# Plain fp32 input and output projections, with seven modulation sums moved into the output projection

## Chip, core and metric

The kernel runs on one core of a Trainium2 chip. The metric is the device time of one execution in microseconds; several executions are timed and their median is taken.

## What is computed

One decoder layer over 256 tokens of width 2048, all in fp32. The parts that matter here, cut from the reference:

```python
mod = (silu(c) @ w_ada + b_ada)            # 6 parts of 2048: sh1, sc1, g1, sh2, sc2, g2
h = rmsnorm(x, norm1_g) * (1 + sc1) + sh1
proj = h @ w_in                            # 2048 -> 3904: sq, sk, sv (1024 each), cq 512, ckv 256, kr 64
sb_out  = stick_breaking_attention(sq, sk, sv)                 # 8 heads of 128
mla_out = mla_attention(rmsnorm(cq) @ w_uq, rmsnorm(ckv) @ w_ukv, kr)   # 8 heads
mixed = concat([rmsnorm(sb_out), rmsnorm(mla_out)]) @ w_o      # 2048 -> 2048
x = x + g1 * mixed
h2 = rmsnorm(x) * (1 + sc2) + sh2
x = x + g2 * peer_ffn(h2, ...)             # top-16 experts of 16384 per head and token
out = rmsnorm(x, final_norm_g)
```

## The kernel before

**Stages.** The order of the work on each engine is written out by hand. TensorE goes through: an opening, in which the first two modulation parts are summed and three column blocks of `w_in` (`cq`, `ckv`, `q0`, named `OPENING`) are multiplied in plain fp32 (L876, L882); the input projection proper, the five blocks `q1`, `k0`, `k1`, `v0`, `v1` of 512 columns each (L892 to L920); the latent products (L923 to L981, among them the plain fp32 products by `contract`, L457); attention, a software pipeline over 16 heads (`JOBS`), whose stages are `scores`, `middle`, `values` and `squares`; the output projection, four blocks `w_o0` to `w_o3` of 512 columns (L1055 to L1092); the query projection (L1134); and then the expert retrieval, which gathers rows of `peer_u` and `peer_v` by index and runs to the end.

**Split products.** In the input and the output projection an fp32 product is made from three fp32r products. A block of 16 chunks of 128 rows is handled in 8 pairs of chunks (`PAIRS`, class `Pair`). For each pair ScalarE casts the weights to fp32r (`make_high`, L448, into `win_high` or `wo_high`, four buffers each), VectorE subtracts that from the whole (`make_low`, L452, in place in the weight ring as `ring_low`), and the activations are parted likewise (`hT_high` L1322 and `hT_low` L1740; `mix_high_part` L1434 and `mix_low_part` L1874). TensorE then multiplies high by high, high by low and low by high: 24 matmuls of 256 columns per pair in `q1`, `k0` and `k1` (L912), 12 of 512 columns in `v0` and `v1` (L906) and in the output projection (L1069).

**Weights.** Block weights go through a ring of two slots of 32 KB per partition, loaded in halves by SyncE's DMA queue. A slot's half is loaded again when its reader has passed a semaphore (`plan_load`, `halves_read`).

**Modulation.** `w_ada` is 96 pieces of 1 MB. The first 32 (two parts) are summed in the opening (`first_step`, L486; pieces of 512 KB through 14 buffers, and SyncE's load of a piece waits for the step that frees its buffer). Pieces 32 to 95 are loaded by GpSimd's queue through three buffers (`ada_late`, L308) and each added on VectorE by one instruction of 128x2048 (`ada_sum`, L322). At the end of a part, TensorE sums it over the partitions with 16 one-column matmuls (`ada_cols`, L333), and VectorE may begin the next part only after these. In the kernel before, pieces 32 to 58 stand between the `make_low` calls of the input projection, 59 to 63 behind it, 64 to 70 (`ADA_IN` is 71) just ahead of attention on VectorE, and 71 to 85 in the output projection: two ahead of its loop, 13 in blocks 1 to 3.

**Rotary table.** VectorE makes the arguments of sine and cosine (L1659 to L1677) in the middle of the first 16 opening steps, and ScalarE's `Sin` (L1262) follows them ahead of the copies of the transposed `x`.

## Time and profile before

| | us |
|---|---|
| median of 3 executions | 1753.91 |
| lowest and highest | 1749.77 and 1756.27 |
| the profiled execution, whole | 1751.18 |
| its span, first to last instruction | 1749.4 |
| TensorE busy in the span | 1478.3 |
| VectorE busy | 1206.5 |
| ScalarE busy | 542.8 |
| GpSimd busy | 690.7 |
| mean granted clock of TensorE | 0.909 of 2.4 GHz |

A row of a timeline gives the start in us from the start of the span, the length in us, the engine, the line of the kernel, the operation, output and inputs by their names in the program, the shapes and the count; in brackets stands how long the engine was idle ahead of it and what ended that. A row of the chain of waits gives a start, a length and what the end of the program waited for in that stretch. The trace keeps two records for a plain fp32 matmul and one for an fp32r matmul; both print as f32. Lengths of matmuls overlap, so a rate is read from one start to the next.

### The profile page before, as it was taken

To read this page: it belongs to the slowest core of one execution; us is meant where nothing else is said; L and a number is where in the kernel's file an instruction comes from. 1 tells how busy PE (TensorE), PEld (TensorE's weight loads), DVE (VectorE), ACT (ScalarE), POOL (GpSimd) and SP (SyncE) were. 2 spreads that over 40 slices of the span, in tenths; PEclk is the share of its full clock that TensorE was granted. 3 is DMA by queue.
4 is the path that set the end of the run, shared out by engine and by line. 5 is a ranking of instruction groups with operands and counts; after the bars stand their busy time and mean duration, and the time that the engine had idled before them with its cause. 6 is when DMAs were issued, how large, how long until landed. Compare 5 with 4: busy or idle time off the path is not lost.

```text
span 1749.4 us, 20157 instructions
## 1 busy us (share of the span) xinstructions
PE 1478.3 (85%) x7320; PEld 980.5 (56%) x7320; DVE 1206.5 (69%) x2134; ACT 542.8 (31%) x1589; POOL 690.7 (39%) x626
## 2 busy tenths in 40 slices
PE   2979999989999998898999757656689899988874
PEld 2558987878788875666676434324333343333331
DVE  5877886879889988898454467768654555445463
ACT  3003442764311247343210146537421010101132
POOL 1000011000122354556676466555654454445461
PEclk9889999999999999999999876667789999998987
DMA  9999997849969679999999899998989999999996
GB/s 337 386 385 407 402 354 308 303 167 370 380 233 359 225 293 379 377 368 397 390 402 396 325 388 379 378 350 319 394 338 406 366 402 400 362 417 389 416 381 249
DMA packets 149806, 624.46 MB, mean 357 GB/s; under 512 B 33994, under 2 KB 38272, under 8 KB 86528
## 3 DMA queue, kind: packets, MB, share of 16 engines
q0 software_dynamic: 82976, 427.52, 62.6%
q1 hardware_dynamic: 66732, 195.67, 29.1%
q8 instruction: 58, 0.95, 0.2%
q14 instruction: 40, 0.33, 0.0%
HBM read 797.54 MB, written 2.10 MB: 457 GB/s over the span
## 4 chain that ended last, share of the span: by engine, by line
PE 31%; DMA 30%; DVE 24%; issue 6%; POOL 5%; ACT 3%; DVEq 1%; SPq 1%; POOLq 0%; ACTq 0%
DMA u_rows<-in_peer_u,expert 23%; DVE u_rows L2033 12%; PE ps L1167 6%; PE ps L1069 5%; PE ps L457 4%; PE ps L912 4%; DVE first_acc L486 3%; DMA v_rows<-in_peer_v,expert_rows 3%; POOL v_rows L801 3%; PE ps L906 2%; PE ps L1219 2%; PE ps L1134 2%; DMA ada_first<-in_w_ada 2%; PE ps L1204 2%; DMA u_rows<-in_peer_v,expert_rows 1%
## 5 line engine op out<-in xcount | busy, mean ns | idle before, releaser
L2033 DVE SCALAR_TENSOR_TENSOR u_rows<-u_rows,h 128x1024 f32<-128x1024 f32 (+1 forms) x416 | 595.3, 1469 | 377.9 <-DMA u_rows<-in_peer_u,expert 374.3
L801 POOL DMA_INDIRECT u_rows<-in_peer_u,expert x256 | 320.6, 1253 | 364.5 <-DVE u_rows L2033 289.5
L801 POOL DMA_INDIRECT v_rows<-in_peer_v,expert_rows x199 | 264.1, 1327 | 162.3 <-PE ps L1167 108.5
L1167 PE MATMUL ps<-v_rows,diag 128*32 128x512 f32 x1592 | 259.4, 693 | 65.1 <-DMA v_rows<-in_peer_v,expert_rows 35.6
L1219 PE MATMUL ps<-dense_rows,dense_weight 128*128 128x512 f32 x640 | 290.6, 612 | 14.9 <-DVE dense_sums L2112 8.2
L457 PE MATMUL ps<-h2T,dense_rows 128*128 128x256 f32 x1280 | 284.0, 383 | 4.2 <-ACT dense_weight L1565 4.1
L457 PEld LDWEIGHTS ps<-h2T,dense_rows 128*128 128x128 f32 x1280 | 243.4, 191 | 52.6 <-issue 17.9
L1219 PEld LDWEIGHTS ps<-dense_rows,dense_weight 128*128 128x128 f32 x640 | 123.1, 196 | 181.9 <-issue 174.9
L1167 PEld LDWEIGHTS ps<-v_rows,diag 128*32 128x32 f32 x1592 | 64.9, 125 | 182.5 <-issue 182.0
L308 POOL DMA_DIRECT2D ada_late<-in_w_ada x61 | 32.4, 531 | 303.7 <-DVE ada_acc L322 260.8
L1204 PE MATMUL ps<-high_hot,low_hot 128*128 128x40 f32 x512 | 82.1, 332 | 78.7 <-issue 54.0
L322 DVE SCALAR_TENSOR_TENSOR ada_acc<-ada_late,cact,ada_acc 128x2048 f32<-128x2048 f32 x57 | 133.8, 2348 | 18.8 <-DMA ada_late<-in_w_ada 17.7
L1167 PE MATMUL ps<-spare_rows,diag 128*32 128x512 f32 x296 | 135.7, 673 | 9.7 <-DMA v_rows<-in_peer_v,expert_rows 9.7
L1204 PEld LDWEIGHTS ps<-high_hot,low_hot 128*128 128x128 f32 x512 | 78.9, 244 | 95.0 <-issue 95.0
L1134 PE MATMUL ps<-h2T,ring 128*128 128x256 f32 x512 | 114.2, 383 | 0.0
L1134 PEld LDWEIGHTS ps<-h2T,ring 128*128 128x128 f32 x512 | 97.4, 192 | 13.0
L1487 ACT ACTIVATE hidden<-hidden 128x16 f32<-128x16 f32 x15 | 3.2, 215 | 314.6 <-DVE hidden L2041 311.5
L1576 ACT ACTIVATE low_hot<-iota,slot_rows 128x128 f32<-128x128 f32 x256 | 78.1, 387 | 41.1 <-PE ps L1204 40.9
L486 DVE SCALAR_TENSOR_TENSOR first_acc<-ada_first,cact,first_acc 128x1024 f32<-128x1024 f32 x60 | 77.0, 1284 | 16.1 <-DMA ada_first<-in_w_ada 10.8
L1509 ACT COPY weight_rows<-kept 32x4 f32<-32x4 f32 x240 | 47.1, 196 | 109.4 <-DVE kept L2058 106.7
L1561 ACT ACTIVATE diag<-ident,weight_rows 128x32 f32<-128x32 f32 x256 | 58.6, 308 | 40.0 <-PE ps L1167 39.4
L448 ACT CAST win_high<-ring 128x1024 fp32r<-128x1024 f32 x40 | 41.8, 1052 | 74.4 <-DMA ring<-in_w_in 32.0
(308 smaller groups left out, 1874.1 us busy)
## 6 DMA issues: line engine op xcount, KB each, us to landing
ada_late<-in_w_ada POOLq DMA_DIRECT2D x61, 1024.0 KB, 7.8
dense_rows<-in_dense_u SPq DMA_DIRECT2D x40, 1024.0 KB, 8.9
dense_rows<-in_dense_v SPq DMA_DIRECT2D x40, 1024.0 KB, 9.0
ada_first<-in_w_ada SPq DMA_DIRECT2D x64, 512.0 KB, 11.6
ring<-in_w_in SPq DMA_DIRECT2D x10, 2048.0 KB, 23.8
ring<-in_w_o SPq DMA_DIRECT2D x8, 2048.0 KB, 16.8
ring<-in_w_peer_q SPq DMA_DIRECT2D x8, 2048.0 KB, 13.8
opened<-in_w_in SPq DMA_DIRECT2D x8, 1024.0 KB, 13.0
```

Source lines behind the costliest of these rows:

```text
L322: nc.vector.scalar_tensor_tensor(out=a, in0=piece, scalar=cact[:, kc:kc + 1], in1=a, op0=ALU.mult, op1=ALU.add).then_inc(ada_steps, 1)
L457: ins = nc.tensor.matmul(half, lhs(k), rhs(k), start=(k == 0), stop=(k == kc - 1))
L486: nc.vector.scalar_tensor_tensor(out=a, in0=piece, scalar=cact[:, kc:kc + 1], in1=a, op0=ALU.mult, op1=ALU.add).then_inc(first_steps, 1)
L801: nc.gpsimd.indirect_dma_start(buf[:, :], None, table, bass.IndirectOffsetOnAxis(ap=places, axis=0), bounds_check=last_sparse, oob_is_err= ...
L912: ins = nc.tensor.matmul(banks[b // 2][:, T * (b % 2):T * (b % 2) + T], w.of(part, k, P * b, P), h[:, ch, :], start=first and b % 2 == 0, ...
L1069: ins = nc.tensor.matmul(banks[t], mixed[:, h, P * t:P * t + P], w.of(part, k), start=h % H == 0 and part is w.high and mixed is mix_high_ ...
L1134: ins = nc.tensor.matmul(bank[:, T * s:T * s + T], ring[item[name][0]][:, lo:lo + P], h2T[:, ch, :], start=(ch == 0 and s == 0), stop=(ch ...
L1167: ins = nc.tensor.matmul(ps[rows, k, :], diag[n % len(diag)][:, :], v_slot(n)[0][:, 512 * k:512 * k + 512], start=first, stop=last)
L1204: ins = nc.tensor.matmul(o, low_hot[i % 2][:, k, :], high_hot[i % 2][:, k, :], start=True, stop=True)
L1219: ins = nc.tensor.matmul(ps[:, 4 + t, :], weight_tile(PIECE * m + a)[:, P * t:P * t + P], rows[:, 512 * a:512 * a + 512], start=m == 0 and ...
L1576: ins = nc.scalar.activation(hot[:, k, :], iota128[:, :], ACT.Abs, scale=-1.0, bias=slot_rows[:, 1, BATCH * b + k:BATCH * b + k + 1])
L2033: ins = nc.vector.scalar_tensor_tensor(out=u_rows[b][:, lo:hi], in0=u_rows[b][:, lo:hi], scalar=1.0, in1=h2[:, q // H, lo:hi], op0=ALU.mul ...
```

## The change

1. **Plain fp32 products.** Class `Pair`, both sets of cast buffers, `ring_low`, the parted activations and all semaphores between them are gone. TensorE reads the ring and `hT` or `mix` directly: 64 matmuls per input block of 256 columns, 32 per block of 512 columns, and it waits itself for the weights' halves.
2. **Modulation.** `ADA_IN` is 64. Pieces 64 to 70 are summed in the output projection: the list of places there grows from 13 to 20 (`(0, 2)` to `(0, 7)` and `(1, 3)` are new). In the input projection the sums stand in a row.
3. **Attention's end.** The pipeline has 20 steps on TensorE, not 22; the squares of the last two heads follow the first two pairs of the output projection.
4. **Rotary arguments** go to the fourth step of the second 16 opening steps (`trig_args`), and `Sin` behind ScalarE's first part of `hT`.

```diff
-    def halves_read(high_read, n, last):
-
-        return (high_read, PAIRS * n + PAIRS // 2 + 1), unit_read(last)
...
-        plan_load(name, n % 2, halves_read(in_high_read, n, f"{name}_1"))
+        plan_load(name, n % 2, ((in_half_read, n + 1), unit_read(f"{name}_1")))
...
-        plan_load(f"w_o{n}", n % 2, halves_read(w_high_read, n, f"w{n}_1_1"))
+        plan_load(f"w_o{n}", n % 2, (unit_read(f"w{n}_0_1"), unit_read(f"w{n}_1_1")))
...
-    ADA_IN, ADA_OUT = 71, 86
+    ADA_IN, ADA_OUT = 64, 86
...
-                for m in range(PAIRS):
-                    w = Pair(name, PAIRS * n + m, m, win_high, width)
...
-                    pe.wait_ge(in_low, w.c + 1)
...
+                w = chunks(name)
+                for ch in range(KC):
+                    if ch % KH == 0:
+                        loaded(pe, name, ch // KH)
...
+                            ins = nc.tensor.matmul(banks[t][:, 0:width], hT[:, ch, P * t:P * t + P], w[:, ch, 0:width],
+                                                   start=(ch == 0), stop=last)
...
+                                ins = nc.tensor.matmul(banks[b // 2][:, T * (b % 2):T * (b % 2) + T],
+                                                       w[:, ch, P * b:P * b + P], hT[:, ch, :],
...
-            for k in range(JOBS + 6):
+            for k in range(JOBS + 4):
...
+                def product(h, t):
+                    ins = nc.tensor.matmul(banks[t], mix[:, h, P * t:P * t + P], w[:, h, :],
+                                           start=(h % H == 0), stop=(h % H == H - 1))
...
+                    if n == 0 and m < 2:
+                        squares(JOBS - 2 + m)
...
             for j in range(4):
                 gained(j)
                 move_h(2 * j)
-                if j:
-                    opened_read_through(dve, j - 1, 2)
-                    h_parted(j - 1)
                 if j < 3:
                     for kc in range(KC):
                         first_step(j + 1, kc)
+                        if j == 0 and kc == 3:
+                            trig_args()
...
-                    if (n, m) in ((1, 0), (1, 1), (1, 2), (1, 6), (1, 7), (2, 0), (2, 1), (2, 6), (2, 7), (3, 0), (3, 1), (3, 2), (3, 3)):
+                    if (n, m) in ((0, 2), (0, 3), (0, 4), (0, 5), (0, 6), (0, 7), (1, 0), (1, 1), (1, 2), (1, 3), (1, 6), (1, 7), (2, 0), (2, 1), (2, 6), (2, 7), (3, 0), (3, 1), (3, 2), (3, 3)):
                         ada_sum(next(ada))
```

Three places in the order of the instructions follow. `ps` is PSUM, a number behind a name is its buffer, `x8` counts like instructions in a row, and brackets hold the semaphores that a row waits for.

TensorE where attention ends and the output projection begins, before (`L1022` and `L1023` are the last values, `L1030` squares, `L1044` the rows of the gate):

```order
L1022 MATMUL ps<-ma_114,vm 128x256
L1023 MATMUL ps<-ma_114,vm 128x128
L1030 MATMUL ps<-ones,sq 128x1 x4
L1069 MATMUL ps<-wo_high_123,mix_high_part 128x512 x2
L1069 MATMUL ps<-wo_high_123,mix_low_part 128x512 x2
L1069 MATMUL ps<-wo_high_123,mix_high_part 128x512 x2
L1069 MATMUL ps<-wo_high_123,mix_low_part 128x512 x2
L1069 MATMUL ps<-ring_low_119,mix_high_part 128x512 x4
```

The same place in the changed kernel:

```order
L974 MATMUL ps<-ma_108,vm 128x256
L975 MATMUL ps<-ma_108,vm 128x128
L1011 MATMUL ps<-ring_49,mix 128x512 x4
L982 MATMUL ps<-ones,sq 128x1 x2
L1011 MATMUL ps<-ring_49,mix 128x512 x4
L982 MATMUL ps<-ones,sq 128x1 x2
L996 MATMUL ps<-ident,modc 128x128 x16
L1011 MATMUL ps<-ring_49,mix 128x512 x24
```

Twelve matmuls of a pair became four, they read the ring and `mix` themselves, and the last squares stand behind the first two pairs.

VectorE ahead of attention, before (`L343` adds the bias of the gate's part, `L1810` is attention's first instruction on this engine):

```order
L343 TENSOR_TENSOR modc<-ps,vcA 128x16 [waits ada_columns,qpe_ready]
L319 TENSOR_SCALAR ada_acc<-ada_late_87,cact 128x2048 [waits ada_columns,ada_late2_loaded]
L322 SCALAR_TENSOR_TENSOR ada_acc<-ada_late_85,cact,ada_acc 128x2048 [waits ada_steps,ada_late0_loaded]
L322 SCALAR_TENSOR_TENSOR ada_acc<-ada_late_86,cact,ada_acc 128x2048 [waits ada_steps,ada_late1_loaded]
L322 SCALAR_TENSOR_TENSOR ada_acc<-ada_late_87,cact,ada_acc 128x2048 [waits ada_steps,ada_late2_loaded]
L322 SCALAR_TENSOR_TENSOR ada_acc<-ada_late_85,cact,ada_acc 128x2048 [waits ada_steps,ada_late0_loaded]
L322 SCALAR_TENSOR_TENSOR ada_acc<-ada_late_86,cact,ada_acc 128x2048 [waits ada_steps,ada_late1_loaded]
L322 SCALAR_TENSOR_TENSOR ada_acc<-ada_late_87,cact,ada_acc 128x2048 [waits ada_steps,ada_late2_loaded]
L1810 SCALAR_TENSOR_TENSOR za_111<-za_111 128x384 [waits bank0_emptied]
L1830 SCALAR_TENSOR_TENSOR za_111<-za_111 128x384 [waits log_term]
```

And in the changed kernel:

```order
L335 TENSOR_TENSOR modc<-ps,vcA 128x16 [waits ada_columns,qpe_ready]
L1721 SCALAR_TENSOR_TENSOR za_105<-za_105 128x384 [waits bank0_emptied]
L1741 SCALAR_TENSOR_TENSOR za_105<-za_105 128x384 [waits log_term]
L1743 TENSOR_TENSOR za_105<-za_105,mask_sb 128x2x128 [waits vector_steps]
L1728 TENSOR_TENSOR ma_107<-ps,mask_mla 128x384 [waits bank1_filled]
```

The seven sums stand no longer between the gate's bias and attention.

VectorE in the changed kernel at the start of the output projection (`L311` is the first sum of the fifth part, the others are sums and the scales of the norm):

```order
L311 TENSOR_SCALAR ada_acc<-ada_late_81,cact 128x2048 [waits ada_columns,ada_late2_loaded]
L314 SCALAR_TENSOR_TENSOR ada_acc<-ada_late_79,cact,ada_acc 128x2048 [waits ada_steps,ada_late0_loaded]
L1824 TENSOR_SCALAR rs_g<-ps 128x4 [waits squares_summed]
L314 SCALAR_TENSOR_TENSOR ada_acc<-ada_late_80,cact,ada_acc 128x2048 [waits ada_steps,ada_late1_loaded]
L314 SCALAR_TENSOR_TENSOR ada_acc<-ada_late_81,cact,ada_acc 128x2048 [waits ada_steps,ada_late2_loaded]
L314 SCALAR_TENSOR_TENSOR ada_acc<-ada_late_79,cact,ada_acc 128x2048 [waits ada_steps,ada_late0_loaded]
L1827 RECIPROCAL rs_g<-rs_g 128x4 [waits grp_norm]
L314 SCALAR_TENSOR_TENSOR ada_acc<-ada_late_80,cact,ada_acc 128x2048 [waits ada_steps,ada_late1_loaded,grp_norm]
L314 SCALAR_TENSOR_TENSOR ada_acc<-ada_late_81,cact,ada_acc 128x2048 [waits ada_steps,ada_late2_loaded]
L314 SCALAR_TENSOR_TENSOR ada_acc<-ada_late_79,cact,ada_acc 128x2048 [waits ada_steps,ada_late0_loaded]
```

Eight sums stand here where the kernel before had two, and no `make_low` is left between them.

## Rows read from the trace of the kernel before

**Rows 1.** The page: span, and the chain that ended last by engine, line.

```profile
span 1749.4 us, 20157 instructions
...
PE 31%; DMA 30%; DVE 24%; issue 6%; POOL 5%; ACT 3%; DVEq 1%; SPq 1%; POOLq 0%; ACTq 0%
DMA u_rows<-in_peer_u,expert 23%; DVE u_rows L2033 12%; PE ps L1167 6%; PE ps L1069 5%; PE ps L457 4%; PE ps L912 4%; DVE first_acc L486 3%; DMA v_rows<-in_peer_v,expert_rows 3%; POOL v_rows L801 3%; PE ps L906 2%; PE ps L1219 2%; PE ps L1134 2%; DMA ada_first<-in_w_ada 2%; PE ps L1204 2%; DMA u_rows<-in_peer_v,expert_rows 1%
```

**Rows 2.** The chain in order of time, 149 to 371 us: start, length, what.

```profile
149.15 66.23 PE ps L912 x552
...
219.22 5.33 PE ps L912 x24
224.55 43.65 PE ps L906 x191
...
363.35 8.13 PE ps L1069 x24
```

**Rows 3.** Stretches: length, busy PE, PEld, DVE, ACT, POOL (count), PEclk, DMA share, GB/s.

```profile
148.80:215.20 66.40, 66.40 (x554) 66.37 (x553) 60.48 (x55) 30.06 (x39) 6.88 (x13) 1.00 1.03 404
...
358.70:374.80 16.10, 12.59 (x66) 10.83 (x65) 11.40 (x13) 11.41 (x17) 1.06 (x2) 0.79 0.35 130
374.80:421.20 46.40, 46.40 (x208) 38.39 (x207) 41.16 (x35) 24.16 (x30) 3.71 (x7) 1.00 0.84 308
...
457.50:1749.40 1291.90, 1078.47 (x5251) 648.95 (x5249) 846.48 (x1728) 366.21 (x1291) 655.24 (x519) 0.89 0.92 361
```

**Rows 4.** Timeline of PE, 271 to 292 us: plain fp32 products, two records each.

```profile
271.03 14.05 PE L457 MATMUL ps<-cqT,ring 128*128 128x256 f32 x64 [0.86 <-ACT cqT L1345]
284.92 7.03 PE L457 MATMUL ps<-ring,cqT 128*128 128x512 f32 x16
291.78 3.63 PE L333 MATMUL ps<-ones,ada_acc 128*128 128x1 f32 x32
```

**Rows 5.** Groups by line, whole span: busy us, mean ns | idle before.

```profile
L1219 PE MATMUL ps<-dense_rows,dense_weight 128*128 128x512 f32 x640 | 290.6, 612 | 14.9 <-DVE dense_sums L2112 8.2 <-DMA dense_rows<-in_dense_v 4.9 <-issue 1.8
...
L1134 PE MATMUL ps<-h2T,ring 128*128 128x256 f32 x512 | 114.2, 383 | 0.0
...
L452 DVE TENSOR_TENSOR ring_low<-ring,win_high 128x1024 fp32r<-128x1024 f32 x40 | 47.9, 1218 | 11.3 <-ACT win_high L448 11.1
...
L452 DVE TENSOR_TENSOR ring_low<-ring,wo_high 128x1024 fp32r<-128x1024 f32 x32 | 38.8, 1219 | 1.9 <-ACT wo_high L448 1.9
```

**Rows 6.** Timeline of PE, 358 to 364 us: the last squares, the first products.

```profile
358.72 1.24 PE L1030 MATMUL ps<-ones,sq 128*128 128x1 f32 x8
363.35 1.19 PE L1069 MATMUL ps<-wo_high,mix_high_part 128*128 128x512 f32 x2 [3.38 <-DVE ring_low L452]
```

**Rows 7.** Timeline of ACT, 310 to 311 us: attention's first copy.

```profile
310.86 0.49 ACT L1363 ACTIVATE za<-ps 128x384 f32<-128x384 f32 x1
```

**Rows 8.** Timeline of DVE, 310 to 313 us: last sum, attention's first.

```profile
310.66 2.35 DVE L322 SCALAR_TENSOR_TENSOR ada_acc<-ada_late,cact,ada_acc 128x2048 f32<-128x2048 f32 x1 [0.43 <-DMA ada_late<-in_w_ada]
312.93 0.55 DVE L1810 SCALAR_TENSOR_TENSOR za<-za 128x384 f32<-128x384 f32 x1
```

**Rows 9.** Timeline of PE, 315 us: its first wait in attention.

```profile
315.79 0.67 PE L1004 MATMUL ps<-za,tri 128*128 128x256 f32 x2 [2.62 <-DVE za L1832]
```

**Rows 10.** Timeline of DVE in the opening, 98 to 123 us.

```profile
98.15 1.28 DVE L1740 TENSOR_TENSOR hT_low<-hT,hT_high 128x512 fp32r<-128x512 f32 x2
...
109.71 13.78 DVE L486 SCALAR_TENSOR_TENSOR first_acc<-ada_first,cact,first_acc 128x1024 f32<-128x1024 f32 x10 [2.60 <-DMA ada_first<-in_w_ada]
```

**Rows 11.** Waits of SyncE's queue, 20 to 130 us: total us, times, longest.

```profile
SPq L472 <- DVE first_acc L486: 34.7, 28, 3.5
```

**Rows 12.** Timeline of POOL: issues of modulation pieces in three stages.

```profile
155.83 0.53 POOL L308 DMA_DIRECT2D ada_late<-in_w_ada  x1 [4.00 <-DVE ada_acc L322]
...
394.09 0.53 POOL L308 DMA_DIRECT2D ada_late<-in_w_ada  x1 [2.87 <-DVE ada_acc L322]
...
477.72 0.53 POOL L308 DMA_DIRECT2D ada_late<-in_w_ada  x1 [1.93 <-DVE ada_acc L322]
```

More of the change, by code:

```diff
@@ L423, in group, with chunks @@
         return loaded(eng, name)[:, 0:kc * width].rearrange("p (kc n) -> p kc n", kc=kc)
[L425 to L452 removed]
+    def chunks(name):
+        return ring[item[name][0]][:, :].rearrange("p (kc n) -> p kc n", kc=KC)
     def contract(half, lhs, rhs, kc):
@@ L1059, in _ @@
                     if m % (PAIRS // 2) == 0:
+                        g = m // (PAIRS // 2)
                         banks = [take(pe, f"w{n}_{g}_{t}") for t in range(TT)]
+                        loaded(pe, f"w_o{n}", g)
+                    pair = (2 * m, 2 * m + 1)
                     if n == 0:
-                        pe.wait_ge(mix_low, 2 * m + 2)
-                    pe.wait_ge(w_low, w.c + 1)
-                    products = [(part, k, mixed) for part, mine in ((w.high, (mix_high_part, mix_low_part)), (w.low, (mix_high_part,)))
-                                for k in range(2) for mixed in mine]
@@ L1067, in product @@
-                    def product(part, k, mixed, t):
-                        h = 2 * m + k
-                        ins = nc.tensor.matmul(banks[t], mixed[:, h, P * t:P * t + P], w.of(part, k),
-                                               start=h % H == 0 and part is w.high and mixed is mix_high_part,
-                                               stop=h % H == H - 1 and part is w.low)
-                        if h % H == H - 1 and part is w.low:
-                            fill(ins, f"w{n}_{g}_{t}")
-                        return ins
@@ L1076, in _ @@
-                    if w.c == 4 * PAIRS - 1:
+                        for h in pair:
+                            copied(pe, f"o{2 * h if h < H else 2 * (h - H) + 1}")
+                    if n == 3 and m == PAIRS - 1:
                         for t in range(TT):
-                            for p in products:
-                                product(*p, t)
+                            for h in pair:
+                                product(h, t)
                     else:
-                        for p in products:
+                        for h in pair:
@@ L1260, in _ @@
                 nc.scalar.activation(xs[:, t, :], xs[:, t, :], ACT.Copy, scale=st[:, 2 + t:3 + t]).then_inc(xs_scaled, 1)
-            act.wait_ge(trig_arg, 1)
-            nc.scalar.activation(trig[:, 5:7, :], trig[:, 2:4, :], ACT.Sin).then_inc(trig_ready, 1)
             for u in range(8):
@@ L1653, in _ @@
             nc.vector.reciprocal(st[:, 2:4], st[:, 2:4]).then_inc(row_rstd, 1)
-            for kc in range(7, 10):
+            for kc in range(7, KC):
                 first_step(0, kc)
-            dve.wait_ge(const_ready, 2)
-            dve.wait_ge(pos_loaded, 16)
-            step(nc.vector.tensor_copy(st[:, 8:10], posi[:, :]))
-            for t in range(TT):
-                v.add(nc.vector.tensor_scalar(trig[:, 1, HALF * t:HALF * t + HALF], trig[:, 0, 0:HALF],
-                                              st[:, 8 + t:9 + t], None, ALU.mult))
```

219 lines of the change are left out of this document (69 added, 150 removed).

## The prediction, made before the changed kernel was run

> **What bounds the kernel now.** I read the page first: of a span of 1749.4 us the chain that ended last has 31% on TensorE, 30% on DMA and 24% on VectorE, and its largest single line, the gathers of `peer_u` (23%), lies in the retrieval, which the change doesn't touch [rows 1]. The lines that it does touch are L1069 (5%), L912 (4%) and L906 (2%). So the question is what ends last in the two projections, and whether what follows moves along.
>
> The chain in order of time answers the first half. From 149.15 us it lies on L912 for 66.23 us without a break, then, behind the one-column sums, on L912 again for 5.33 us and on L906 for 43.65 us [rows 2]. The stretches say the same: 66.40 of 66.40 us busy in the first, 46.40 of 46.40 us in the middle of the output projection, both at clock 1.00 (2.4 GHz) [rows 3]. Neither VectorE (60.48 of 66.40 us busy) nor DMA (share 1.03) stops TensorE there, though both are nearly full. Both projections are bound by TensorE's own instruction stream.
>
> The second half: from 457.5 us on there are 1291.9 us in which all begins with the experts chosen from the output projection's result; the DMA queues carry the same instructions in the same order in both kernels. I take this part to move as a block.
>
> **Plain products on TensorE.** Before: 552 records of L912 are 23 pairs in 66.23 us, 2.88 us a pair; 24 such pairs are 69.1 us. L906 has 16 pairs in 43.65 us, 2.73 a pair [rows 2]. The output projection's middle, 374.80 to 421.20 us, is the third to the nineteenth pair, 17 in 46.40 us (17 x 12 matmuls, and a few records that reach over the ends), 2.73 a pair, so 32 are 87.3 us [rows 3]. Sum 200.1 us.
>
> After: the same plain products stand in the trace already, at full clock. With weights standing and 256 columns moving, 64 records start at 271.03 and the next form starts at 284.92: 13.89 / 64 = 0.217 us a record. With 512 columns, 16 records from 284.92 to 291.78 give 0.429 us [rows 4]. A matmul has two records. `q1`, `k0`, `k1`: 3 x 64 matmuls, 384 records, 83.3 us. `v0`, `v1`: 2 x 32 matmuls, 128 records, 54.9 us. Output projection: 4 x 32 matmuls, 256 records, 109.8 us. Sum 248.0 us, so **+47.9 us** (14.2 + 11.2 + 22.5), all of it on the chain. Bounds: the busy time of two large groups gives 0.223 us for 256 columns (114.2 / 512) and 0.454 us for 512 (290.6 / 640) [rows 5], which would add 2.3 and 9.7 us. I take the low ones, because they are continuous runs at full clock with the same operands' shapes, and keep 12 us for the range. No row lies below.
>
> The Trainium skill, "FP8 and Floating Point Precision", section "TensorE Precision Notes", says that true fp32 takes four passes through the array. By it, a pair would go from three passes to four, a third more than 200.1 us, or +66.7 us; the rows above say +47.9, since the fp32r matmuls here take 0.120 us for 256 columns where half a plain record takes 0.109. That is the third rival.
>
> **Work taken from VectorE and ScalarE.** 72 makings of low parts, 47.9 + 38.8 us on VectorE [rows 5], and as many casts on ScalarE go. They lie beside TensorE and are worth nothing while it is the bound; they are worth something in three places:
>
> 1. *Attention to output projection.* TensorE ends its last squares at 359.96 and starts L1069 at 363.35, having waited 3.38 us for a low part, which stood behind two sums and an activation part on VectorE [rows 6]. In the changed kernel the first products need `w_o0`, long loaded, and head outputs of the first two heads: **-3.4 us**. In that stretch the clock is 0.79, part of it at 1.2 GHz, after one-column matmuls and the wait [rows 3]; the first two pairs take 8.13 us instead of 5.46 [rows 2]. Without the wait the products follow at once on other matmuls: **-2.7 us**, between 0 and that, since the one-column matmuls stay. The squares' 1.24 us stay too, two pairs later.
> 2. *Into attention.* Seven sums leave VectorE. The last of them ends and attention's first instruction starts at 312.93, though ScalarE had its input ready at 310.86 + 0.49 = 311.35 [rows 7, 8]: **-1.6 us**. The upper bound is TensorE's wait, 2.62 us [rows 9]. The remainder of attention is untouched.
> 3. *Opening.* Two parts of `hT_low`, each some 1.3 us, stood in VectorE's row before the last sums [rows 10], and SyncE's loads waited 28 times for those sums [rows 11], so the saving could come through, at most 2.6 us. But in the last round VectorE itself waited 2.60 us for a piece, and then ran ten without a gap. The moved rotary arguments change places inside the same rounds. I take **-1.0 us**, range 0 to -2.6.
>
> **The seven moved sums.** Each is 2.35 us on VectorE [rows 8] and one DMA of 1 MB on GpSimd's queue; the order of that queue is unchanged. In the output projection VectorE now has 20 sums, 47 us, and the residuals, beside 109.8 us of TensorE: hidden. The first that waits for them is `ada_cols(4)`, in the 19th pair, 19 x 3.43 = 65 us after the start, with 16 sums due. At 3.40 us a piece (0.53 + 2.87), the pace of this stage before, they take 54 us; at 2.46 us, the pace with little other traffic, 39 us [rows 12]. Cost nothing; if the cover fails it is the second rival. In the input projection, 16 sums are due after 22 pairs (76 us), the other 16 about 85 us later: slack at every pace seen. TensorE's own new waits for weight halves: a slot is free for two blocks' halves some 27 us before it is read again, at 2 MB a half.
>
> **Sum.** 47.9 - 3.4 - 2.7 - 1.6 - 1.0 = +39.2 us. The profiled execution took 1751.2 us, so 1790.4; the median of the three runs is 2.7 us above it. I forecast **1791**, nearer to the profiled one. Ends of the terms: +47.9 - 3.4 - 2.7 - 2.6 - 2.6 = +36.6 (1788), and +47.9 + 12.0 - 3.4 = +56.5 (1808). The three runs spread over 6.5 us, and the retrieval's waits may fall otherwise by a few us, which widens the low end more than the mechanism does.
>
> **Rivals.**
>
> *Modulation late.* For: in the input stage pieces came every 4.53 us (0.53 + 4.00) [rows 12] while DMA was full. At that pace 16 sums take 72.5 us against 65 on TensorE, a wait of 7 us at `ada_cols(4)`: 1798. Against: DMA share is 0.84 there, not 1.03 [rows 3].
>
> *A plain pass costs as much as a split one.* 200.1 x 4/3, so +66.7 - 8.7 = +58.0: 1809. For: the L1219 group at 0.454. Against: [rows 4] show the plain forms directly.
>
> *The delay is absorbed (the other side).* If what ends the program were a stream that doesn't wait for the projections, such as SyncE's dense tiles, the 47.9 us would vanish in its slack, and the savings of 8.7 us would stay: 1742. It decides from the point where more than 39 us of slack lies behind the output projection. For: DMA share is 0.92 over the last 1291.9 us [rows 3]. Against: on the chain stand the gathers (23%) and their dot products (12%), which wait for the experts, and no dense tile [rows 1].
>
> **Chances.** Forecast 0.82, modulation late 0.07, plain pass dear 0.06, absorbed 0.02, partly absorbed to within 0.5% (8.8 us, about what a measurement of this kernel can tell from no change) 0.03. So faster 0.02, same 0.03, slower 0.95. The range for 8 in 10 is 1780 to 1808: the forecast with its bounds, the modulation rival and the runs' spread; the dear pass lies just outside.
>
> **What the changed profile would show.** L864 (256 columns) in records 0.217 us apart and L858 and L1011 (512 columns) 0.429 apart, TensorE without idle time in both; input projection about 145 us long instead of 119, output projection about 119 instead of 98; L1011 starting straight behind the last values near 381 us; attention's first VectorE instruction within 0.2 us of ScalarE's copy; the last 1292 us as long as before. Wrong if TensorE waits for `ada_acc` at L325 in the output projection, if records are 0.45 apart, if the clock in the projections falls under 1.00, or if the part behind the output projection changes length by more than 5 us.

## The result, and the profile after

| | before | after |
|---|---|---|
| median, us | 1755.09 (4 runs) | 1795.66 (4 runs) |
| lowest and highest | 1749.77 and 1756.32 | 1791.08 and 1798.97 |
| ratio, 95% interval | | 1.0235 [1.0201, 1.0269] |
| profiled execution, its span | 1751.18, 1749.4 | 1793.51, 1791.8 |

The changed kernel is 2.3% slower. The forecast was 1791 us, its range 1780 to 1808. The page of the changed kernel answers [rows 1]:

```profile
span 1791.8 us, 19168 instructions
...
PE 1526.0 (85%) x6936; PEld 946.7 (53%) x6936; DVE 1118.1 (62%) x2046; ACT 465.1 (26%) x1501; POOL 707.1 (39%) x626
...
PE 37%; DMA 27%; DVE 21%; issue 6%; POOL 4%; ACT 2%; DVEq 1%; SPq 0%; POOLq 0%; ACTq 0%
DMA u_rows<-in_peer_u,expert 20%; DVE u_rows L1935 11%; PE ps L1116 6%; PE ps L1011 6%; PE ps L417 5%; PE ps L864 5%; PE ps L1168 4%; DMA v_rows<-in_peer_v,expert_rows 3%; PE ps L858 3%; DVE first_acc L446 3%; POOL v_rows L758 3%; DMA ada_first<-in_w_ada 3%; PE ps L1083 2%; PE ps L1153 2%; DVEq L1855 1%
```

TensorE's share of the chain that ended last rose from 31% to 37%. VectorE and ScalarE did 88 and 78 us less work, and next to nothing of it shows in the time. The gathers and their dot products stand first in the chain, as before.

The chain in order of time, answering [rows 2] (start, length, what; L864 is `q1`, `k0`, `k1`, L858 `v0` and `v1`, L417 the latent products, L325 one-column sums, L1011 the output projection):

```profile
150.22 79.43 PE ps L864 x368
229.65 3.46 PE ps L325 x32
233.12 5.25 PE ps L864 x16
238.36 54.95 PE ps L858 x128
295.65 20.92 PE ps L417 x80
316.57 4.26 PE ps L325 x32
320.82 16.45 PE ps L417 x48
...
385.49 3.44 PE ps L1011 x8
...
396.83 58.37 PE ps L1011 x136
455.19 3.47 PE ps L325 x32
458.66 43.00 PE ps L1011 x96
```

79.43 / 368 = 0.216 us a record of 256 columns, 54.95 / 128 = 58.37 / 136 = 0.429 us a record of 512: the prices that the plain products of the kernel before had shown [rows 4]. TensorE goes from one piece to the next without idle time. The last L1011 row, 43.00 / 96 = 0.448, is dearer, and so are the 48 records of L417 behind 316.57.

The stretches, as [rows 3] (length, busy PE, PEld, DVE, ACT, POOL with counts, granted clock, DMA share, GB/s):

```profile
150.00:229.50 79.50, 79.50 (x371) 69.97 (x370) 32.65 (x29) 8.83 (x19) 6.89 (x13) 1.00 0.96 373
229.50:238.20 8.70, 8.70 (x49) 7.79 (x48) 4.84 (x4) 0.59 (x1) 1.06 (x2) 0.80 0.24 79
...
320.80:337.30 16.50, 16.50 (x51) 11.06 (x51) 0.17 (x1) 4.11 (x8) 0.00 (x0) 0.85 0.00 0
...
396.70:455.00 58.30, 58.30 (x138) 25.81 (x137) 37.87 (x26) 6.24 (x13) 6.89 (x13) 1.00 1.02 393
455.00:462.00 7.00, 7.00 (x38) 5.11 (x37) 3.12 (x2) 0.00 (x0) 0.53 (x1) 0.78 0.57 189
...
506.00:1791.80 1285.80, 1073.10 (x5230) 644.52 (x5228) 844.45 (x1724) 366.64 (x1289) 671.60 (x519) 0.90 0.92 362
```

The clock is 1.00 while the long rows of products run, and falls behind each group of one-column sums: 0.80, 0.85, 0.78. The part behind the output projection is as long as before (1285.8 us; before, 1291.9 us from 457.5 on, of which the first 3.6 are still products).

The places where something was to be saved, in the changed kernel: TensorE's first products of the output projection, ScalarE's first copy of attention, and VectorE's first instruction there (start, length, engine and line, operation; idle time in brackets):

```profile
385.33 3.60 PE L1011 MATMUL ps<-ring,mix 128*128 128x512 f32 x8
```

```profile
338.82 0.49 ACT L1302 ACTIVATE za<-ps 128x384 f32<-128x384 f32 x1
```

```profile
339.35 0.56 DVE L1721 SCALAR_TENSOR_TENSOR za<-za 128x384 f32<-128x384 f32 x1 [18.24 <-ACT za L1302]
```

No bracket stands behind L1011: it starts straight behind the last values. In the chain its eight records take 3.44 us, which is 0.430 a record, at full clock; where it stands, [rows 6] have a wait of 3.38 us. VectorE's first instruction follows ScalarE's copy (338.82 + 0.49) by 0.04 us, where it came 1.58 us late [rows 7, 8].

To compare all kernels I use five marks of TensorE and VectorE, each the start of a row: first product of `q1` and first product of the output projection (as the chain has them; the timeline starts some plain rows 0.16 us earlier), first latent product, attention's first VectorE instruction, and the transposes (L1099 before, L1048 after) with which the last part, mostly the retrieval, begins.

| kernel | input | latent | attention | output | last part | span | last part's length |
|---|---|---|---|---|---|---|---|
| before | 149.15 | 271.03 | 312.93 | 363.35 | 466.30 | 1749.4 | 1283.1 |
| after | 150.22 | 295.65 | 339.35 | 385.49 | 511.03 | 1791.8 | 1280.8 |
| e7, after again | 149.88 | 295.30 | 338.98 | 385.08 | 510.61 | 1799.5 | 1288.9 |
| e1, input plain | 149.12 | 294.55 | 335.93 | 386.39 | 492.94 | 1776.3 | 1283.4 |
| e2, output plain | 147.68 | 268.00 | 310.04 | 356.06 | 481.60 | 1763.6 | 1282.0 |
| e3, sums back | 149.25 | 294.68 | 338.36 | 384.38 | 509.92 | 1797.9 | 1288.0 |
| e4, sums moved alone | 149.48 | 269.79 | 311.83 | 361.54 | 473.66 | 1760.3 | 1286.6 |
| e6, columns spread | 149.60 | 293.33 | 333.69 | 379.78 | 503.62 | 1795.3 | 1291.7 |
| e11, split and lean | 149.68 | 268.51 | 310.56 | 358.89 | 460.86 | 1742.9 | 1282.0 |

By these marks the last part begins 44.7 us later in the changed kernel, in four pieces: opening +1.1, input projection +23.5, latent products +1.8, attention -4.3, output projection +22.6. It then takes 2.3 us less, which makes the 42.4 us between the spans.

### The profile page after: what moved, and what is told of

The parts are those of the page before. It is cut to its first block, busy times and chain, and to the rows that moved or that the text cites. A ratio compares the mean times of both kernels' runs of the same rounds, so it can differ in the third digit from the quotient of the medians.

```text
span 1791.8 us, 19168 instructions
## 1 busy us (share of the span) xinstructions
PE 1526.0 (85%) x6936; PEld 946.7 (53%) x6936; DVE 1118.1 (62%) x2046; ACT 465.1 (26%) x1501; POOL 707.1 (39%) x626
## 3 DMA queue, kind: packets, MB, share of 16 engines
q0 software_dynamic: 82976, 427.52, 60.9%
## 4 chain that ended last, share of the span: by engine, by line
PE 37%; DMA 27%; DVE 21%; issue 6%; POOL 4%; ACT 2%; DVEq 1%; SPq 0%; POOLq 0%; ACTq 0%
DMA u_rows<-in_peer_u,expert 20%; DVE u_rows L1935 11%; PE ps L1116 6%; PE ps L1011 6%; PE ps L417 5%; PE ps L864 5%; PE ps L1168 4%; DMA v_rows<-in_peer_v,expert_rows 3%; PE ps L858 3%; DVE first_acc L446 3%; POOL v_rows L758 3%; DMA ada_first<-in_w_ada 3%; PE ps L1083 2%; PE ps L1153 2%; DVEq L1855 1%
## 5 line engine op out<-in xcount | busy, mean ns | idle before, releaser
L758 POOL DMA_INDIRECT u_rows<-in_peer_u,expert x256 | 327.1, 1278 | 351.8 <-DVE u_rows L1935 274.3
L758 POOL DMA_INDIRECT v_rows<-in_peer_v,expert_rows x199 | 269.9, 1356 | 154.6 <-PE ps L1116 100.5
L1168 PE MATMUL ps<-dense_rows,dense_weight 128*128 128x512 f32 x640 | 287.7, 607 | 16.1 <-DVE dense_sums L2014 10.1
L417 PE MATMUL ps<-h2T,dense_rows 128*128 128x256 f32 x1280 | 284.3, 383 | 3.8 <-ACT dense_weight L1498 3.8
L417 PEld LDWEIGHTS ps<-h2T,dense_rows 128*128 128x128 f32 x1280 | 243.4, 191 | 52.8 <-issue 19.1
L1116 PE MATMUL ps<-spare_rows,diag 128*32 128x512 f32 x296 | 139.0, 685 | 11.2 <-DMA v_rows<-in_peer_v,expert_rows 11.2
L1011 PE MATMUL ps<-ring,mix 128*128 128x512 f32 x256 | 112.6, 600 | 0.0
L446 DVE SCALAR_TENSOR_TENSOR first_acc<-ada_first,cact,first_acc 128x1024 f32<-128x1024 f32 x60 | 77.1, 1284 | 20.0 <-DMA ada_first<-in_w_ada 14.6
L864 PE MATMUL ps<-hT,ring 128*128 128x256 f32 x384 | 85.0, 385 | 0.0
L1011 PEld LDWEIGHTS ps<-ring,mix 128*128 128x128 f32 x256 | 48.8, 192 | 59.9 <-issue 59.9
```

The source lines that it names most:

```text
L417: ins = nc.tensor.matmul(half, lhs(k), rhs(k), start=(k == 0), stop=(k == kc - 1))
L446: nc.vector.scalar_tensor_tensor(out=a, in0=piece, scalar=cact[:, kc:kc + 1], in1=a, op0=ALU.mult, op1=ALU.add).then_inc(first_steps, 1)
L758: nc.gpsimd.indirect_dma_start(buf[:, :], None, table, bass.IndirectOffsetOnAxis(ap=places, axis=0), bounds_check=last_sparse, oob_is_err= ...
L864: ins = nc.tensor.matmul(banks[b // 2][:, T * (b % 2):T * (b % 2) + T], w[:, ch, P * b:P * b + P], hT[:, ch, :], start=(ch == 0 and b % 2 ...
L1011: ins = nc.tensor.matmul(banks[t], mix[:, h, P * t:P * t + P], w[:, h, :], start=(h % H == 0), stop=(h % H == H - 1))
L1116: ins = nc.tensor.matmul(ps[rows, k, :], diag[n % len(diag)][:, :], v_slot(n)[0][:, 512 * k:512 * k + 512], start=first, stop=last)
```

## The experiments

The first four were run together, with 13 runs of the kernel before (median 1755.31).

**e1, the plain products in the input projection only, and e2, in the output projection only.** Each is one side of the change; the seven sums stay ahead of attention, and e1 has the changed opening too. Both cuts are against the kernel before. In e1:

```diff
-                for m in range(PAIRS):
-                    w = Pair(name, PAIRS * n + m, m, win_high, width)
+                w = chunks(name)
+                for ch in range(KC):
```

In e2:

```diff
-            for k in range(JOBS + 6):
+            for k in range(JOBS + 4):
...
-                for m in range(PAIRS):
-                    w = Pair(f"w_o{n}", PAIRS * n + m, m, wo_high)
+                w = chunks(f"w_o{n}")
```

> Opening, input projection and latent stage as in the changed kernel, the output projection, its split products and the place of the seven modulation sums as in the kernel before. Theory (each projection costs what its plain products cost, and adds): input projection 143 us long instead of 119.5, output projection 102 as before, whole time 24 us above the kernel before (1779). Rival (the two parts share one slack, so that one alone costs little): under 10 us above. Rival (delay absorbed later): stage 24 us longer, whole time not.

> Only the output projection is made of plain products, with the last squares behind its first two pairs; input projection and the seven sums as before. Theory: from the last values to the last product 120 us instead of 102, whole time 17 to 18 us above the kernel before (1773); TensorE doesn't wait for VectorE where the projection starts (3.4 us before). With e1 the sum is the whole change less some 2 us. Rival: the saving at the start is larger than the plain products cost, and the time stays.

Measured: e1 1776.23 us, ratio 1.0138 [1.0087, 1.0190]; e2 1770.05 us, 1.0122 [1.0074, 1.0170]. From the five marks: the input projection takes 145.4 us in every kernel that has all its plain products and the one-column sums in a row, and 120.3 us in e2 and e4, +25.1 where I had worked out +25.4 (14.2 + 11.2). Against the trace of before it is only +23.5, because there a stretch behind the one-column sums ran slow: 3.84 and 5.33 us, in e2 and e4 3.47 and 4.47. In e2 the output projection is 125.5 us long, as in the changed kernel, and the way from attention to it 46.0 us instead of 50.4 (46.1 in the changed kernel). In e1 the output projection, whose code is that of before, takes 106.6 us instead of 103.0; 3.2 of it lie at and behind the third group of one-column sums (4.42 and 35.03 us, before 3.47 and 32.81), a slow stretch again. Apart from these stretches both sides behave alone as they do together. What follows: the cost is TensorE's stream, and it doesn't depend on the other side. The two spans lie 26.9 and 14.2 us above the span of before, 41.1 together, where the whole change has 42.4; by the ratios it is about 24 and 21 us, each with some 9 either way.

**e3, the changed kernel with the seven sums back ahead of attention, and e4, the kernel before with only these moved.**

```diff
-    ADA_IN, ADA_OUT = 64, 86
+    ADA_IN, ADA_OUT = 71, 86
```

(in e3; in e4 the other way round, each with the list of places that belongs to it)

> The changed kernel with the seven sums ahead of attention again. Theory: attention's first instruction on VectorE comes 1 to 3 us later behind ScalarE's copy, nothing else; whole time +1.6 us, inside the noise. Rival (the moved sums delay the output projection): the output projection gets shorter than 120.5 us and the whole time falls.

> The kernel before with only the seven sums moved into the first blocks of the output projection, between the makings of low parts. Theory: VectorE has 3.1 + 2.35 us a pair there against 2.73 us of TensorE, so TensorE now waits: six sums in block 0 and one in block 1, up to 7 x 2.35 = 16 us less the lead it has, some +8 to +14 us, minus 1.6 at attention's start. Rival (sums are hidden wherever they stand): -1.6 us.

Measured: e3 1798.20 us, ratio 1.0266 [1.0223, 1.0309]; e4 1764.07 us, 1.0053 [1.0021, 1.0085]. The 1.6 us of e3 are not there: VectorE's first instruction of attention in e3 stands behind seven sums and is on time all the same (timeline of VectorE, 290 to 345 us).

```profile
338.36 0.56 DVE L1721 SCALAR_TENSOR_TENSOR za<-za 128x384 f32<-128x384 f32 x1 [1.16 <-ACT za L1302]
```

It even waits 1.16 us for ScalarE. The reason is a slow stretch of TensorE behind the one-column sums of the latent stage, in e3 as in the changed kernel: ScalarE's first copy is done 43.7 us after the first latent product in the changed kernel and 40.3 us after it in the kernel before (311.35 - 271.03), so the sums fit in. In the changed kernel their move bought nothing. In e1, which has the same plain input projection, the same latent stage and the seven sums ahead of attention, the stretch is not slow (48 records in 13.9 us), and there the sums do delay attention, by 1.06 us. The timelines of e1, ScalarE's first copy and VectorE's first instruction:

```profile
334.38 0.49 ACT L1344 ACTIVATE za<-ps 128x384 f32<-128x384 f32 x1
```

```profile
335.93 0.55 DVE L1769 SCALAR_TENSOR_TENSOR za<-za 128x384 f32<-128x384 f32 x1
```

In the kernel before it costs. Moved alone, the sums free VectorE for attention (at 311.83 it has waited 17.37 us for ScalarE's copy). Even so attention starts no earlier behind the first latent product, 42.0 us against 41.9, because the 48 records there took 15.58 us instead of 13.90; e2, with the sums ahead of attention and the same 15.58 us, has 42.0 too. And the output projection grows from 102.95 to 112.1 us. Its stretches, first of before and then of e4:

```profile
363.40:392.00 28.60, 28.60 (x132) 24.03 (x133) 20.88 (x22) 17.42 (x23) 1.06 (x2) 0.91 0.40 150
392.00:424.00 32.00, 32.00 (x156) 26.94 (x155) 29.86 (x26) 14.74 (x19) 2.65 (x5) 1.00 1.04 384
```

```profile
361.50:392.00 30.50, 30.16 (x140) 24.82 (x140) 30.41 (x25) 19.22 (x26) 3.71 (x7) 0.94 0.77 280
392.00:424.00 32.00, 27.22 (x108) 19.57 (x108) 30.27 (x23) 11.63 (x15) 3.71 (x7) 1.00 1.05 396
```

Up to 392 VectorE is busy 30.41 of 30.50 us; after that TensorE, which had 32.00 of 32.00, has 27.22. Per pair VectorE has a sum (2.35 us), a low part of the weights (1.22) and one of `mix` (0.69), 4.0 us from one `make_low` to the next (starts overlap a little), and TensorE's pair takes 2.73. The last part begins 7.4 us later, inside what was expected. So the moved sums need the plain products, which take the `make_low` calls away.

The second batch (e5 to e8; 17 runs of before, median 1753.66) asks what lies close behind TensorE and where the clock goes.

**e5, part of the products of `v0` and `v1` left out.**

```diff
-                    last = ch == KC - 1
+                    last = ch == (KH if name[0] == "v" else KC - 1)
+                    if name[0] == "v" and ch > KH:
+                        continue
```

> The changed kernel with seven of the sixteen chunks left out of the products of v0 and v1 (56 records of 512 columns; the loads stay). It asks whether something stands close behind TensorE. Theory (TensorE alone bounds the input projection, and what follows moves as a block): 56 x 0.429 = 24 us less, both in the stage and in the whole time. Rival (VectorE's sums or the weight loads are close behind): TensorE waits for w_in or at the columns of the third modulation part, and less than 15 us are gained.

Measured: 1791.3 us, 1.0207 [1.0163, 1.0251]. This looks like the rival: of 24 us hardly more than 4 arrived in the medians. But the marks say otherwise. The last part begins at 487.60 us, 23.4 earlier than in the changed kernel, and then takes 1300.4 us, 19.6 more. The page gives the reason for part of that: the gathers' queue (queue, packets, MB, share) in the changed kernel, and then in e5:

```profile
q0 software_dynamic: 82976, 427.52, 60.9%
```

```profile
q0 software_dynamic: 82976, 431.01, 61.8%
```

With other values in `v` other experts are chosen, and 3.49 MB more are gathered; at the 362 GB/s of the last part that is some 10 us. The experiment changed two things at once. e9 and e10 below repeat it with the data held equal.

**e6, the one-column sums set singly between products** (in the changed kernel, all three groups of the projections and the latent stage; the cut shows the one of the output projection):

```diff
-                    if n == 2 and m == 2:
-                        ada_cols(4)
+                                if n == 2 and 2 <= m < 6:
+                                    ada_col(4, 4 * (m - 2) + 2 * (h - 2 * m) + t)
```

> The changed kernel with the 16 one-column matmuls of the modulation parts 3, 4 and 5 placed singly between 16 products instead of in a row. Theory (the granted clock falls to 1.2 GHz behind a row of one-column matmuls): no stretch under 1.00 in the input projection, the latent stage and the output projection; their products run 0.217 and 0.429 us a record throughout; 1.8 + 3.4 + 1.8 = 7 us less in the stages. Rival (the falls come from elsewhere, such as the phase of the clock's own steps): the falls stay at the same places or move, and the time stays.

Measured: 1793.17 us, 1.0218 [1.0175, 1.0261]. The stretches of e6 over the latent stage and over the output projection are at full clock, as is its input projection (149.60 to 291.00 us, 1.00):

```profile
293.30:335.00 41.70, 41.54 (x182) 31.03 (x183) 5.46 (x14) 11.43 (x21) 0.00 (x0) 1.00 0.19 70
391.10:495.00 103.90, 103.90 (x274) 48.37 (x273) 57.91 (x44) 10.24 (x22) 10.07 (x19) 1.00 0.93 354
```

The last part begins at 503.62 us, 7.4 earlier than in the changed kernel (1.7 in the input projection, 3.3 in the latent stage, 1.7 in the output projection, 0.6 in the opening): what was expected. The median moved by 2.5 us, since the last part was 1291.7 us long in this execution. Four executions of each can't tell 7 us from 2.

**e7, the changed kernel once more**, for one profile.

> The changed kernel once more, to see which of the falls of the granted clock repeat. Theory (a row of one-column matmuls may or may not bring it down, as it falls): other places than in the first trace, each 1.5 to 3.5 us; stage lengths otherwise equal to 0.5 us.

Measured: 1801.35 us, span 1799.5. All five marks lie within 0.5 us of those of the first profile, the slow stretches included (the second group of one-column sums took 4.53 us here and 4.26 there, the 48 records behind it 16.16 and 16.45). The last part is 8.1 us longer. So the expectation, falls at other places, missed: they stand at the same places. Everything up to the retrieval repeats to half a microsecond, and the retrieval doesn't repeat to eight, with the same data and the same 427.52 MB. Cut into tenths, some have a little less granted clock (0.71 against 0.74 in the fifth) or fewer bytes moved (368 against 372 GB/s there, 388 against 395 in the eighth) than in the first profile; no single place holds the 8 us.

**e8, the kernel before with every saving of the change that doesn't need plain products:** a start with high by high, later squares, spread columns, and 16 sums in the output projection.

```diff
+                    if w.c == 0:
+                        pe.wait_ge(mix_high, 2)
+                        pe.wait_ge(w_high, 1)
...
-    ADA_IN, ADA_OUT = 71, 86
+    ADA_IN, ADA_OUT = 70, 86
```

> The kernel before, with split products, and four small changes: the first pair of the output projection starts with high by high, before the low parts; the two sums ahead of its loop and the sum of piece 70 stand later; the last squares follow the first two pairs; one-column matmuls stand singly between products. Theory: TensorE starts the output projection some 2.3 us earlier, no half-clock pair there or in the input projection (2.7 + 2.4 us), 1 us at attention's start: 7 to 9 us under the kernel before, about 1747. Rival: VectorE, which is nearly full in blocks 0 and 1, gives it back; no change.

Measured: 1763.19 us, 1.0052 [1.0028, 1.0076], a miss with the wrong sign. The last part begins at 474.26 us, 8.0 later than in the kernel before. Timeline of VectorE in e8, ahead of attention and at the start of the output projection:

```profile
299.40 1.29 DVE L319 TENSOR_SCALAR ada_acc<-ada_late,cact 128x2048 f32<-128x2048 f32 x1
...
314.06 0.55 DVE L1833 SCALAR_TENSOR_TENSOR za<-za 128x384 f32<-128x384 f32 x1
```

```profile
371.67 0.16 DVE L1943 TENSOR_SCALAR rs_g<-ps 128x4 f32<-128x4 f32 x1 [5.20 <-PE ps L1042]
```

Spreading the columns of part 3 over the latent products puts their end, and with it the first sum of the next part, from 295.63 to 299.40 (from 24.6 to 31.5 us behind the first latent product, which starts at 267.90 here); attention then waits for VectorE until 314.06, though ScalarE's copy started at 307.73. And the squares that were put two pairs later hold VectorE for 5.20 us in front of the low parts of the third pair. In the kernels with plain products both are harmless: no `make_low` stands behind the squares, and in e6 no sums stand between the columns of part 3 and attention, where VectorE waits 8.78 us for ScalarE.

The last batch (17 runs of before, median 1753.14):

**e9 and e10, a cut with equal data.** In both `v0` and `v1` are summed from chunk 7 on. e9 multiplies chunks 0 to 6 and throws them away; e10 doesn't multiply them.

```diff
-                                                   start=(ch == 0), stop=last)
+                                                   start=(ch in (0, KH - 1)), stop=(last or ch == KH - 2))
```

```diff
+                    if name[0] == "v" and ch < KH - 1:
+                        continue
```

> The changed kernel with all its products, but in v0 and v1 the sums are started anew at chunk 7, so that the first 7 of 16 chunks are multiplied and their part of v is left out of the result. TensorE has exactly the work of the changed kernel; only the data behind v0 and v1 differ, and so the experts chosen. It is the partner of the next run. Theory (the part-v run lost its gain because other experts were chosen, with 3.48 MB more to gather): the stages up to the expert retrieval as long as in the changed kernel, within 1 us; more megabytes on the gathers' queue than 427.52, and the part behind the output projection 8 to 20 us longer: about 1805 to 1815. Rival (the gain was lost to a stream that doesn't wait for the projections): 1794 to 1798, the same as the changed kernel.

> The changed kernel without the products of chunks 0 to 6 in v0 and v1 (their part of v is left out of the result; all loads stay). It computes the same values as the run before it, and TensorE has 56 records of 0.429 us less to do, 24.0 us. Theory (nothing close behind TensorE, the rest moves as a block): 20 to 24 us below the run before it, 24 less up to 3.3 for the wait for the latent weights seen in the part-v run. Rival (a stream independent of the projections ends next): less than 8 us below it.

Measured: e9 1801.84 us, 1.0278 [1.0250, 1.0306]; e10 1783.00 us, 1.0168 [1.0140, 1.0196]. e9 missed its own expectation: it gathers 427.70 MB, only 0.18 more than the changed kernel, and its last part is 1287.3 us long, inside the scatter of the others. What counts is the pair. e10's last part begins at 487.25 us against 510.88: 23.6 us earlier, where 24.0 were taken out. Not all of that is the cut itself: the input projection is 21.6 us shorter, the opening 0.4, and 1.6 come from the latent stage, where the one-column sums and the 48 records behind them took 19.04 us instead of 20.71. The waits of TensorE in e10 from 148 to 511 us (line, for what: total, times, longest) show what lies next behind it:

```profile
PE ps L860 <- DMA ring<-in_w_in: 1.4, 1, 1.4
...
PE ps L417 <- DMA ring<-in_w_uq: 1.4, 1, 1.4
```

These are the weights, for which the changed kernel shows no wait at all in this stretch. By the medians 18.8 us remain (the ratios give 19 us, with some 7 either way), by the spans 17.4; the last part of e10 is 1293.6 us long, and whether that is more than its scatter can't be said from one profile. The rival (less than 8 us) is out. e5's last part is 6.8 us longer than e10's, with 3.3 MB more gathered; that the bytes are the reason is argued (3.3 MB at 362 GB/s would be 9 us, an estimate), not shown.

**e11, e8 without its two faults:** high by high first; columns of parts 2 and 4 spread, those of part 3 left together; squares where they were; two sums taken from ahead of the first low part into the third and fifth pair.

```diff
-            ada_sum(next(ada))
-            ada_sum(next(ada))
...
-                    if (n, m) in ((1, 0), (1, 1), (1, 2), (1, 6), (1, 7), (2, 0), (2, 1), (2, 6), (2, 7), (3, 0), (3, 1), (3, 2), (3, 3)):
+                    if (n, m) in ((0, 2), (0, 4), (1, 0), (1, 1), (1, 2), (1, 6), (1, 7), (2, 0), (2, 1), (2, 6), (2, 7), (3, 0), (3, 1), (3, 2), (3, 3)):
```

> The kernel before with three small edits: the first pair of the output projection begins with high by high, which needs no low part; the one-column sums of the parts 2 and 4 stand singly between products; and two modulation sums leave the place ahead of the first low part for the third and fifth pair. The squares stay where they were. Theory: the start of the output projection gains 2 to 2.7 us of the 3.38 waited, the two groups of one-column sums 1.7 us each (as in the changed kernel with spread sums), some half-speed pairs up to 2.7: the retrieval starts 5 to 8 us earlier than in the kernel before (466.3), and the median is 1746 to 1750. Rival (VectorE has no room for two sums in block 0): TensorE waits for ring_low there, and the retrieval starts no earlier than 465.

Measured: 1745.93 us (12 runs), 0.9965 [0.9946, 0.9985]. It beats both kernels; against the one before by 0.35%, less than the 0.5% that I called the bound, but its interval leaves 1 out. The last part begins 5.4 us earlier than before. Timeline of TensorE at the start of the output projection in e11, and its stretch around the one-column sums of the input projection:

```profile
358.89 2.05 PE L1083 MATMUL ps<-wo_high,mix_high_part 128*128 128x512 f32 x4 [1.30 <-ACT wo_high L457]
```

```profile
212.90:224.00 11.10, 11.10 (x90) 10.78 (x89) 4.24 (x6) 2.34 (x3) 0.08 (x1) 1.00 1.02 381
358.90:366.00 7.10, 7.10 (x26) 5.77 (x27) 7.10 (x8) 7.07 (x10) 0.00 (x0) 0.78 0.00 0
```

The wait went from 3.38 to 1.30 us, now for ScalarE's cast, and the clock stays at 1.00 through the sums of the input projection. At the start of the output projection it is still 0.78, and the first 24 records take 7.13 us (8.13 before). By the marks the input projection is 3.1 us shorter than before, attention 2.1 and the output projection 1.0; of the 3.1 us, e2 and e4 have 1.6 without this edit, so not all of the gain is shown to be the edits'.

## Why the prediction was right, point by point

**The bound and the plain products: right.** TensorE's stream bounded both projections and the records cost 0.216 and 0.429 us. In the input projection the 25.4 us worked out are found as +25.1 (e2, e4 against the plain kernels). From first to last product it took 143.1 us, where 145 were named. The output projection grew by 22.6 us, and that this is so near to the 22.5 of its products is luck: -2.7 at the first pairs, +0.8 for the squares and +1.8 in a slow stretch cancel. TensorE never waited in either, and for its new waits for weight halves the trace shows none. The rival of the dear pass wanted a third more than 200.1 us. The Trainium skill, "FP8 and Floating Point Precision", section "TensorE Precision Notes", with its four passes for true fp32, is the rule behind that rival; the third more is an estimate from it. The trace agrees only in direction: by the rates of the rows above, 384 x 0.216 + 54.95 + 256 x 0.429 = 247.7 us stand against 200.1, 24% more and not 33%, since a pass of an fp32r product took 0.120 us here and half a plain record 0.108.

**Start of the output projection: the mechanism right, the size nearly.** No wait (-3.4) and full clock at the first pairs (-2.7), as the 3.44 us of the first eight records show. The squares came back between the pairs, as said, but smaller than the 1.24 us: both pairs with them took 7.7 us, 0.8 more than 16 x 0.429.

**What I had not in the sum: clock falls later on.** Behind `ada_cols(3)` the latent products took 16.45 us where they had taken 13.90 in the trace of before, and behind `ada_cols(4)` 96 records took 43.00 us where 41.2 are due at 0.429. That is +3.3 (with the sums themselves) and +1.8. One of my signs of being wrong, the clock in the projections under 1.00, was thereby met (0.80 and 0.78 in the stretches above), and the mean of 0.448 us in the last long row comes from it and not from the price of a record: from 463.00 us on the clock is 1.00 again. The sign was badly chosen, since the trace of before has such a fall in its input projection too (24 records of L912 in 5.33 us [rows 2], where 2.88 are due). I had priced only the half-speed stretch at the start of the output projection and taken all other groups of one-column sums to go on as in the trace of before. The runs show that what follows such a group varies between kernels with the same instructions there. The same 48 records take 13.90 us in e5, 15.58 in e2, e4 and e10, and 16.45 in the changed kernel; e1 and e3 run the same instructions on TensorE up to there and take 13.9 and 16.15.

**Into attention, -1.6: the step that failed.** VectorE no longer comes late, but that bought nothing (e3): by the marks the latent stage grew to 43.7 us from 41.9, and the sums would have fitted. The term was right about VectorE's row and wrong in holding TensorE's side fixed, which took 3.3 us more, all of it at and behind the one-column sums. Where it doesn't, the sums cost 1.06 us (e1) or 1.58 (before).

**Opening, -1.0: not found.** It came out at +1.1. VectorE's last ten opening steps, answering [rows 10]:

```profile
110.35 13.79 DVE L446 SCALAR_TENSOR_TENSOR first_acc<-ada_first,cact,first_acc 128x1024 f32<-128x1024 f32 x10 [2.68 <-DMA ada_first<-in_w_ada]
```

They start 0.64 us later than before, still behind a wait for a piece, though 1.3 us of VectorE's work ahead of them is gone. VectorE's savings became waiting: ahead of its opening steps it idles 20.0 us in the changed kernel, 14.6 of them for pieces, and 16.1 and 10.8 before. The eight profiles with the changed opening have 17.6 to 20.0 us, the five with the old one 15.1 to 17.0, and their marks lie at 149.1 to 150.2 and at 147.7 to 149.7. So the saving isn't there, and anything under 2 us here is not to be read from one trace. What sets the pace of the pieces was not tried, nor were the moved rotary arguments alone.

**The seven sums, at nothing: right.** TensorE didn't wait at L325 in the output projection. The sum of VectorE's work there was short by two, 22 sums and not 20 (two stand ahead of the loop), 52 us and not 47, which changes nothing beside 120 us of TensorE. e4 shows what the cover is worth: 9 us without the plain products.

**The rest moves as a block: right in direction, within its scatter.** In ten profiles with unchanged data (the nine of the table, and e8 with 1288.2) the last part is 1280.8 to 1291.7 us long, with no clear order by its start. My criterion, a change of more than 5 us would refute the block, was tighter than the kernel repeats: the first profile is 2.3 us under the one of before, and e7, the very same program, 5.8 over it, which would have met it.

**The sum.** Forecast +39.2 against +42.4 of span and +40.6 of median. Opening (+2.1 over forecast), latent stage (+3.4, clock and the missing saving together), attention (-0.9, the squares that left it), output projection (+2.8: 1.8 for the clock, 0.8 for the squares) and input projection (-1.9) against the trace, and the last part (-2.3) add up to the 3.2 us. The mechanism, 47.9 us of plain products on a bound TensorE, was right; that the sum came so near is in part luck, since misses of +8.3 and -5.1 us cancel.

## What to carry to other kernels

An engine's saved work is worth what its successor waits for: 87 us of VectorE's work removed here bought a wait of 3.4 us and a later place for seven sums, which was worth nothing, and cost 48 us of TensorE, which was the bound. Price an added pass from a continuous run of the same form in the trace, and check moves of work alone as well as together, since a move can be free only because of its companion (e4). When an experiment leaves computation out, hold the data of all that follows equal (e9 and e10), or count the bytes.

## What was not expected of the hardware

- The granted clock fell behind groups of 16 one-column matmuls (32 records, 3.5 us) to 0.78 to 0.85 over the next stretch, part of it at 1.2 GHz (0.51 of 2.4 GHz from 320.80 to 326.00 us in the changed kernel, then 1.00), in some kernels and not in others for the same instructions: 13.90, 15.58 or 16.45 us for 48 records of L417. With the same columns set singly or in fours between products it stayed at 1.00 (e6, e11). What decides it otherwise was not tried.
- Two executions of one program agree within 0.5 us over the first 511 us and differ by 8 us over the next 1285. In a part bound by gathers a difference of 5 us in one profile says nothing.
- A changed value far ahead of a gather by computed index changes the traffic: 3.49 MB more in e5, 0.18 in e9.
